# Weight slabs of the first MoE expert placed outside the ring, and an early index spread for the second expert's gather

## The chip, the cores and the metric

The program runs on one NeuronCore of a Trainium2 chip. The metric is the device time of one execution in microseconds (us), the median of the runs shown. The engines are TensorE (PE in the rows; PEld is its weight load), VectorE (DVE), ScalarE (ACT), GpSimd (POOL) and SyncE (SP), which issues the plain DMAs.

## The reference

One decoder block on 512 tokens of width 1024, all in float32. Two attention mixers (NSA and FoX, 8 heads of 64 each) are gated, mixed, projected by `w_out` and added to `x`. Behind them stands a mixture of 32 experts, of which each token takes 4:

```
x = x + mixed @ w_out
h = rms_norm(x, norm2_g)
logits = h @ router_w + router_b          # 32 experts, the 4 best per token, softmax over the 4
hc = h[tokens of e] @ w1[e] + b1[e]       # w1[e] is 1024 x 2048
act = (clip(up) + 1) * gate * sigmoid(1.702 * gate)
y = (act @ w2[e] + b2[e]) * weight        # w2[e] is 1024 x 1024
x = x + sum over the 4 experts of y;  out = rms_norm(x, norm_f_g)
```

All 32 experts are used, so their weights (8.4 MB and 4.2 MB each, 403 MB together) are all read from HBM.

## The kernel before

The kernel is written by hand: each engine has its own instruction list, and semaphores order them. Nothing is scheduled by a planner.

**Stages.** Projections and the two mixers fill the first 440 us. Then eight chunks of mixed heads are gated into `mixT`; PE multiplies them by `w_out` (L1633, eight halves `u` of 512 columns, two for each of the four token tiles `t`), DVE adds `x` (`add_x`, L2109), and the router, the choice of experts and the numbering of slots follow tile by tile. Each expert has room for 96 tokens (`CAP`) in three groups of 32 (`NG`); its first weight is multiplied in `up` (L1673), its second in `down` (L1682 and L1691).

**Weights.** A weight slab is 1 MB (128 x 2048 floats); a pair of slabs is one DMA of 2 MB, issued by SP in `load_pair(e, u)` (L669). `u` = 0 to 3 are the first weight, 4 and 5 the second. They go to the ring, which has places for six pairs. Earlier stages use the ring too: places 4 and 5 hold `w_out` until the last of its matmuls (`out_full`). The first expert uses places 0 to 3 for its first weight; the second expert uses 4, 5, 2 and, as pair (1, 3), the tile `xs` (`RESIDUAL`), which is free once the residual rows are stored; second weights go to places 0 and 1. Pairs are named (expert, u) below, experts counted from 0. A load waits until PE has used what its place held: `w1_used` counts the eight slabs of a first weight, `w2_used` the four steps of a second one. SP issues in the order of its list, and a load that waits holds all behind it.

**The first expert** runs in two passes (`first_expert`), because its first 64 slots come from the first three token tiles: a pass over two groups while the last tile is still being routed, and a pass over the third group. Between the eight steps `c` of the passes PE does routing work: `count_earlier`, `fill_table` (a table of slot, token and gate parts, by one-hot matmuls, L1585; the last tile's in three parts for experts 0 to 3, 4 to 15, 16 to 31), `turn_first_x` (L1625) and `spread_slots` (L1658), which spreads the slot table over the 128 partitions for the gathers.

**The second expert** (`expert(1, 1)`) may start when `rows_ready` and `xT_ready` say so. Its input comes by this chain:

```
DVE take_parts (L2208, L2209)  slot table out of PSUM, after all three parts of the table
PE  spread_slots (L1658)       in the second pass, behind step c = 1
DVE take_quarters (L2194)      indices of all 32 experts
POOL now_gather (L906), gathered (L911), three indirect DMAs of 128 rows x 1 KB
DVE take_x (L2304, L2306)      transpose and scale, then xT_ready
```

On DVE `count_extra` (L2276 to L2292) and `take_gates` (L2214 to L2199, its last instruction gives `rows_ready`) stand between `take_quarters` and `take_x`. Behind them comes DVE's part of the first expert, `expert(0, 0, None)` (L2315 to L2311). From the third expert on, PE's work repeats in one form: `up` of expert e, then `down` of expert e - 1.

Of the kernel before, what the change touches and what calls it, by code (L numbers as in the profile page):

```python
# [7 lines left out]
F32 = mybir.dt.float32  # L8
# [7 lines left out]
P = 128  # L16
S = 512
# [129 lines left out]
def hybrid_block(nc, x, positions, norm1_g, w_in, cmp_pos_emb, cmp_w1, cmp_w2, fox_f_bias, w_proj_nsa,  # L147
                 w_proj_fox, w_out, norm2_g, router_w, router_b, expert_w1, expert_b1, expert_w2,
                 expert_b2, norm_f_g, rope_freqs, out):
    with ExitStack() as ctx:  # L150
# [41 lines left out]
        mix_f = mixT[:, :, :].rearrange("p a b -> p (a b)")  # L192
        probs = mix_f[:, 0:2 * P_LEN].rearrange("p (a b) -> p a b", a=2)
# [26 lines left out]
        pT = sb("pT", [P, 2, P_LEN])  # L220
        pT_f = pT[:, :, :].rearrange("p a b -> p (a b)")
# [7 lines left out]
        rope_cos = sb("rope_cos", [P, S])  # L229
        rope_sin = sb("rope_sin", [P, S])  # L230
# [96 lines left out]
        table_d = nc.dram_tensor("table", (S + 1, D), F32, kind="Internal").ap()  # L327
        x2_d = nc.dram_tensor("x2", (S + 1 + CAP, D), F32, kind="Internal").ap()
# [11 lines left out]
        xn2 = hT_f.rearrange("p (t d) -> p t d", t=NT)  # L340
# [32 lines left out]
        zero_sb = hT_f[0:CAP, 3 * D:4 * D]  # L373
# [68 lines left out]
        RESIDUAL = 6  # L442
        W1_FIRST, W1_SECOND, W1_LATER = (0, 1, 2, 3), (4, 5, 2, RESIDUAL), (4, 5, 2, 3)
        W2_SLOTS, W2_LAST = (0, 1), W1_LATER[0:2]

        def pair_slot(k):

            return xs_f if k == RESIDUAL else ring[:, 2 * k:2 * k + 2, :].rearrange("p c n -> p (c n)")

        def w1_slots(e):  # L450

            return {0: W1_FIRST, 1: W1_SECOND}.get(e, W1_LATER) if isinstance(e, int) else W1_LATER
# [9 lines left out]
        def up_slab(k, h, j):  # L462

            return slab(k, h).rearrange("p (n j m) -> p n j m", n=2, j=4)[:, :, j, :]
# [37 lines left out]
        now_ready = sem("now_ready")  # L502
        xg_loaded = [sem("xg_loaded%d" % b) for b in range(2)]
# [36 lines left out]
        def _(sp):  # L540
# [1948 lines left out]
```

## Time and profile before

| | |
|---|---|
| runs | 1569.91, 1569.84, 1567.62 us; median 1569.84 |
| profiled execution | 1568.18 us, of which the span of the profile is 1566.4 us |
| mean granted TensorE clock | 0.99 of full speed |
| PE busy | 97% of the span |
| DVE, ACT, POOL busy | 38%, 14%, 19% |
| DMA | 464.25 MB, mean 296 GB/s over the span |

The share of a queue or engine is an average over stages with different limits. The span in 40 slices of 39 us shows two parts: up to about 520 us the DMA engines are lightly used, from about 600 us on their share is 0.9 or more in nearly all slices to the end.

### The profile page before, as it was taken

The page shows a single profiled execution, that of the slowest core. Times are in us where ns is not written, and L with a number is a line of the kernel's source. Part 1 is how long each engine was busy: PE and PEld are TensorE (multiplying, and loading weights), DVE is VectorE, ACT ScalarE, POOL GpSimd, SP SyncE. Part 2 cuts the span into 40 slices and gives each one's busy share as a digit, 9 for nine tenths or more (in the row PEclk, how much of TensorE's full clock was granted, in tenths as well). Part 3 has the DMA queues.
Part 4 walks back from the last instruction along what each step waited for, and adds up shares of the span by engine and source line. Part 5 has one row for each costly group of instructions (what it writes and reads, how often), then busy time and mean ns, then how long its engine had stood idle before and what let it go on. Part 6 is the DMA issues. An engine that isn't in the chain of part 4 may idle for free.

```text
span 1566.4 us, 30553 instructions
## 1 busy us (share of the span) xinstructions
PE 1514.1 (97%) x12602; PEld 673.6 (43%) x12603; DVE 595.5 (38%) x1113; ACT 219.2 (14%) x468; POOL 303.0 (19%) x382
## 2 busy tenths in 40 slices
PE   7999999999999989999999999999999999999993
PEld 4655555666445423333333334555553333333331
DVE  4104555333225544235323432442244323432242
ACT  4212444223212100000000000000000000000001
POOL 2000001432100111212222221222121212222111
PEclk9999999999999999999999999999999999999997
DMA  8122130521271699999999999999999999999994
GB/s 240 27 55 54 40 81 14 179 80 31 66 266 68 236 362 398 414 415 420 417 411 418 420 420 412 417 419 416 414 419 417 415 414 417 415 418 408 417 367 138
DMA packets 109421, 464.25 MB, mean 296 GB/s; under 512 B 33683, under 2 KB 72547, under 8 KB 84546
## 3 DMA queue, kind: packets, MB, share of 16 engines
q1 hardware_dynamic: 95506, 446.82, 70.8%
q0 software_dynamic: 13872, 16.83, 4.6%
q8 instruction: 30, 0.49, 0.1%
q14 instruction: 13, 0.11, 0.0%
HBM read 452.94 MB, written 19.29 MB: 301 GB/s over the span
## 4 chain that ended last, share of the span: by engine, by line
PE 77%; DMA 18%; issue 2%; DVE 1%; ACT 1%; ACTq 0%; DVEq 0%; PEld 0%; SPq 0%; PEldq 0%; POOLq 0%
PE ps L1673 32%; DMA ring<-in_expert_w 17%; PE ps L1259 12%; PE ps L1682 10%; PE ps L1409 7%; PE ps L1691 5%; PE ps L1633 4%; PE ps L1394 2%; PE ps L1371 2%; PE ps L1381 2%; ACT mixT L1089 1%; PE ps L1549 0%; DMA xs<-in_x 0%; PE ps L1271 0%; PE ps L1585 0%
## 5 line engine op out<-in xcount | busy, mean ns | idle before, releaser
L1673 PE MATMUL ps<-ring,oT_fox 128*32 128x512 f32 x6096 | 666.7, 594 | 12.2 <-issue 7.8
L1673 PEld LDWEIGHTS ps<-ring,oT_fox 128*32 128x32 f32 x6096 | 225.2, 110 | 427.8 <-issue 396.0
L2315 DVE TENSOR_TENSOR mixT<-ps,mask 128x768 f32<-128x768 f32 x64 | 61.1, 954 | 577.1 <-PE ps L1673 577.1
L1682 PE MATMUL ps<-ring,hT 128*32 128x512 f32 x2048 | 272.3, 592 | 1.3 <-DMA ring<-in_expert_w 1.1
L1691 PE MATMUL ps<-ring,hT 128*32 128x256 f32 x2048 | 163.0, 379 | 0.0
L1691 PEld LDWEIGHTS ps<-ring,hT 128*32 128x32 f32 x2048 | 78.3, 110 | 141.1 <-issue 140.7
L1409 PE MATMUL ps<-hT,ring 128*128 128x512 f32 x304 | 137.2, 598 | 0.0
L911 POOL DMA_INDIRECT oT_nsa<-table,pc x93 | 105.3, 1133 | 47.1 <-POOL pc L906 27.7
L1189 ACT ACTIVATE mixT<-mixT 128x768 f32<-128x768 f32 x32 | 27.1, 846 | 623.5 <-DVE mixT L2319 623.5
L1682 PEld LDWEIGHTS ps<-ring,hT 128*32 128x32 f32 x2048 | 77.1, 110 | 49.8 <-issue 17.5
L1259 PE MATMUL ps<-hT,ring 128*128 128x512 f32 x208 | 90.4, 593 | 0.0
L906 POOL COPY pc<-pc 128x3 int32 (+1 forms) x31 | 8.6, 278 | 412.8 <-DMA x<-hT,v_win 383.6
L1409 PEld LDWEIGHTS ps<-hT,ring 128*128 128x128 f32 x304 | 55.5, 191 | 64.0 <-issue 64.0
L1199 ACT ACTIVATE hT<-pT,v_fox 128x512 f32<-128x512 f32 (+1 forms) x62 | 34.8, 608 | 310.5 <-DVE pT L2351 310.5
L919 POOL COPY v_win<-v_win 128x1 int32 (+1 forms) x64 | 10.2, 186 | 271.8 <-ACT hT L1199 255.6
L931 POOL DMA_INDIRECT x<-hT,v_win x32 | 52.1, 1628 | 42.6 <-POOL v_win L919 25.5
L1089 ACT ACTIVATE mixT<-ps,st 128x128 f32<-128x128 f32 (+1 forms) x96 | 49.1, 536 | 78.3 <-DVE st L1955 78.3
L1259 PEld LDWEIGHTS ps<-hT,ring 128*128 128x128 f32 x208 | 39.1, 190 | 47.7 <-issue 47.6
L1633 PE MATMUL ps<-ring,mixT 128*128 128x512 f32 x128 | 59.4, 602 | 0.0
L2304 DVE STREAM_TRANSPOSE oT_fox<-oT_nsa 128x768 f32<-128x768 f32 x31 | 49.4, 1592 | 11.1 <-DVE mixT L2323 6.6
L924 POOL DMA_INDIRECT x<-hT,v_win x32 | 50.3, 1572 | 9.8 <-issue 9.8
L2311 DVE STREAM_TRANSPOSE hT<-mixT 128x768 f32<-128x768 f32 x32 | 51.1, 1597 | 1.1
(305 smaller groups left out, 1127.3 us busy)
## 6 DMA issues: line engine op xcount, KB each, us to landing
ring<-in_expert_w SPq DMA_DIRECT2D x189, 2048.0 KB
ring<-in_w_in SPq DMA_DIRECT2D x28, 512.0 KB, 4.9
ring<-in_w_out SPq DMA_DIRECT2D x8, 512.0 KB, 9.0
ring<-in_expert_w SPq DMA_DIRECT2D x4, 1024.0 KB, 24.6
ring<-in_w_in SPq DMA_DIRECT2D x1, 2144.0 KB, 12.9
xs<-in_x SPq DMA_DIRECT2D x4, 512.0 KB, 5.5
ring<-in_w_in SPq DMA_DIRECT2D x8, 256.0 KB, 3.5
ring<-in_w_proj_nsa SPq DMA_DIRECT2D x16, 128.0 KB, 2.8
```

The source lines that it names most:

```text
L911: pool.indirect_dma_start(out=xg_rows[b][:, 256 * g:256 * g + 256], out_offset=None, in_=table_quarter, in_offset=bass.IndirectOffsetOnAxi ...
L924: pool.indirect_dma_start(out=x2_quarter, out_offset=bass.IndirectOffsetOnAxis(ap=now_quarter[b], axis=0), in_=yb[b][:, 512:768], in_offse ...
L931: pool.indirect_dma_start(out=x2_half, out_offset=bass.IndirectOffsetOnAxis(ap=now_half[b], axis=0), in_=yb[b][:, 0:512], in_offset=None, ...
L1089: last = act.activation(probs[:, h, P_OFF[t]:P_OFF[t] + P * (t + 1)], scores(h, t), ACT.Exp, bias=ngm[:, h, t:t + 1], accum_out=sums[:, h, ...
L1259: last = pe.matmul(dst, lhs(c), rhs(c), start=(c == 0), stop=(c == n - 1))
L1409: ins = pe.matmul(w, w_c(c), hT[:, c, :], start=(c == 0), stop=(c == NK - 1))
L1633: ins = pe.matmul(ps[:, u, :], mixT[:, k, t * P:(t + 1) * P], w_o[k][:, n * 512:(n + 1) * 512], start=(k == 0), stop=(k == NK - 1))
L1673: ins = pe.matmul(wide(ps[TG * j:TG * j + TG, hc + g, :]), xT[b][:, g, c, :], up_slab(slots[c // 2], c % 2, j), start=(c == 0), stop=(c == ...
L1682: ins = pe.matmul(ps[TG * q:TG * q + TG, bank, :], gT[b][:, q // 2, c, :], rows[:, at:at + 512], start=(c == 0 and bank == Y_BANK), stop=( ...
L1691: ins = pe.matmul(ps[TG * q:TG * q + TG, bank, 0:256], gT[b][:, 2, c, :], rows[:, at:at + 256], start=(c == 0 and bank == Y_BANK + 1), sto ...
L2311: return dve.transpose(gT[b], act_b.rearrange("p g (m c) -> p g c m", c=NK))
L2315: return dve.tensor_tensor(to, half, b_up[:, 256 * n:256 * n + 256].unsqueeze(1).broadcast_to([P, NG, 256]), ALU.add)
```

## The change

- Slabs 4 to 7 of the first expert's first weight no longer go to ring places 2 and 3, but, as four single loads of 1 MB (`load_lone`), to the second half of `hT`, to a new tile `rope_pT` (it holds the rope tables and `pT`, which lay apart before), to half of `mixT` and to half of `xs`. The arrival of each is told by a semaphore that an early stage had used.
- Pairs (1, 2) and (1, 3) go to the ring places 2 and 3 so freed, behind pair (0, 1). (1, 3) no longer uses `xs`. The waits for earlier loads that stood before pairs (1, 0) and (1, 3) are gone. The loads of the third expert all wait for the second expert's use; (2, 3) was loaded ahead of that before.
- `mixT` is laid out by token tile, so that half of it is free after four of the eight halves. `xn2` has two buffers of a tile in place of four. The zero rows behind `table` and `x2` are gone, with the memset and the two small stores that made them.
- `take_parts`, `spread_slots` and `take_quarters` are each cut in two: for experts 0 to 3 in the first pass, once the table's first part is there, and for the others in the second pass as before.
- On DVE the order behind the second `take_quarters` is `take_x`, `take_gates`, a wait for the first expert's last slab, `count_extra`, `expert(0, ...)`.

```diff
+        mix_t = mix_f.rearrange("p (t k m) -> p t k m", t=NT, k=NK)
...
-        pT = sb("pT", [P, 2, P_LEN])
-        pT_f = pT[:, :, :].rearrange("p a b -> p (a b)")
+        rope_pT = sb("rope_pT", [P, 2 * S + 2 * P_LEN])
+        rope_cos, rope_sin = (rope_pT[:, S * n:S * n + S] for n in range(2))
+        pT_f = rope_pT[:, 2 * S:]
...
-        RESIDUAL = 6
-        W1_FIRST, W1_SECOND, W1_LATER = (0, 1, 2, 3), (4, 5, 2, RESIDUAL), (4, 5, 2, 3)
+        W1_FIRST, W1_LATER = (0, 1, 2, 3), (4, 5, 2, 3)
...
+        FIRST_SLABS = slabs_of(W1_FIRST[0:2]) + [hT_f[:, 2 * D:4 * D], rope_pT[:, 0:2 * D], mix_f[:, 0:2 * D], xs_f[:, 0:2 * D]]
+        LONE = 4
...
+            def load_lone(c):
+                src = expert_w1[0].rearrange("e (p c) n -> e p c n", p=P)[0, :, c, :]
+                sp.dma_start(FIRST_SLABS[c], src).then_inc(lone_loaded[c - LONE][0], 16)
...
             load_pair(0, 0)
+            load_lone(4)
+            sp.wait_ge(bias_turned, 1)
+            load_lone(5)
             sp.wait_ge(mix_sig, NK)
-            for u in range(1, 3):
-                load_pair(0, u)
+            load_pair(0, 1)
+            load_pair(1, 2)
             sp.wait_ge(mix_full, NK)
-            load_pair(0, 3)
-            for t in range(NT - 1):
+            load_pair(1, 3)
+            for t in range(EARLY):
                 store_x2(t)
                 store_table(t)
+                if t == 1:
+                    sp.wait_ge(out_full, 4)
+                    load_lone(6)
+                    sp.wait_ge(x2_stored, 16 * 2)
+                    load_lone(7)
             sp.wait_ge(out_full, 2 * NT)
-            for u in range(2):
-                sp.wait_ge(slabs_loaded[u], 16)
             load_pair(1, 0)
-            store_table(NT - 1)
-            store_x2(NT - 1)
+            store_table(EARLY)
+            store_x2(EARLY)
             load_pair(1, 1)
-            sp.wait_ge(x2_stored, 16 * (NT + 1))
-            sp.wait_ge(slabs_loaded[3], 16)
-            sp.wait_ge(xg_loaded[0], 32)
-            load_pair(1, 3)
             for u in range(2):
                 sp.wait_ge(w1_used, 2 * u + 2)
                 load_pair(0, NK // 2 + u)
-            sp.wait_ge(w1_used, 6)
-            load_pair(1, 2)
-            sp.wait_ge(w1_used, 8)
-            sp.wait_ge(slabs_loaded[3], 32)
-            load_pair(2, 3)
-            for u in range(3):
-                sp.wait_ge(w1_used, NK + 2 * u + 2)
-                load_pair(2, u)
...
+            load_w1(2)
             load_w2(1)
...
-            def spread_slots():
-
+            def spread_slots(n):
+
+                first, end = ((0, HOT_PARTS[EARLY][0][1]), (HOT_PARTS[EARLY][0][1], E))[n]
+                pe.wait_ge(parts_taken, n + 1)
...
                     if 4 <= c <= 6:
                         fill_table(EARLY, c - 4)
+                    if c == 5:
+                        spread_slots(0)
                     if c == 6:
                         turn_first_x(1)
...
                     if c == 1:
-                        pe.wait_ge(parts_taken, 1)
-                        spread_slots()
+                        spread_slots(1)
...
             take_first(1)
+            take_parts(0)
             mark(EARLY, 1)
             shift(EARLY)
             mark(EARLY, 2)
+            take_quarters(0)
             dve.tensor_copy(count, routed(EARLY, 2)).then_inc(count_taken, 1)
-            take_parts()
+            take_parts(1)
             take_first_x(1)
...
             weigh(EARLY)
-            take_quarters()
+            take_quarters(1)
+            take_x(1, 1, gather)
+            take_gates()
+            dve.wait_ge(w1_used, NK)
             count_extra()
-            take_gates()
-            take_x(1, 1, gather)
             expert(0, 0, None)
```

Two places in the order of the instructions. A number after a name is the line, `x` the number of instructions of the form.

PE, the end of the first expert's first pass and its second pass, before (`ring` is the weight slab, L1658 is `spread_slots`, L1625 `turn_first_x`, L1585 and L1598 the table):

```order
L1585 MATMUL ps<-v_sel,qk 96x1 x12
L1673 MATMUL ps<-ring,oT_fox 32x512 x8
L1585 MATMUL ps<-v_sel,qk 96x1 x16
L1625 MATMUL ps<-ident,oT_nsa 128x32 x8
L1673 MATMUL ps<-ring,oT_fox 32x512 x16
L1658 MATMUL ps<-v_fox,ident 32x32 x12
L1673 MATMUL ps<-ring,oT_fox 32x512 x12
L1595 MATMUL ps<-kT_win,qk 96x96
L1598 MATMUL ps<-v_sel,qk 96x3 x32
```

and with the change (L1676 is `up`, L1661 `spread_slots`, L1626 `turn_first_x`, L1586 and L1599 the table):

```order
L1586 MATMUL ps<-v_sel,qk 96x1 x4
L1676 MATMUL ps<-rope_pT,oT_fox 32x512 x8
L1586 MATMUL ps<-v_sel,qk 96x1 x12
L1661 MATMUL ps<-v_fox,ident 32x4 x12
L1676 MATMUL ps<-mixT,oT_fox 32x512 x8
L1586 MATMUL ps<-v_sel,qk 96x1 x16
L1626 MATMUL ps<-ident,oT_nsa 128x32 x8
L1676 MATMUL ps<-xs,oT_fox 32x512 x8
L1676 MATMUL ps<-ring,oT_fox 32x512 x8
L1661 MATMUL ps<-v_fox,ident 32x28 x12
L1676 MATMUL ps<-ring,oT_fox 32x512 x8
L1676 MATMUL ps<-hT,oT_fox 32x512 x4
```

A spread of 12 matmuls with 4 columns now stands ahead of the last two steps of the first pass; the old one stays in its place with 28 columns, and the slabs come from `hT`, `rope_pT`, `mixT` and `xs`.

DVE, behind the choice for the last tile, before (L2174 marks one-hots, L2208 and L2209 are `take_parts`, L2194 `take_quarters`, L2276 the start of `count_extra`):

```order
L2174 TENSOR_TENSOR qk<-kT_win 128x1152
L2142 TENSOR_SCALAR kT_sel<-kT_sel,v_win 128x32
L2174 TENSOR_TENSOR qk<-kT_win 128x1536
L2256 COPY kT_win<-ps 128x32
L2208 COPY v_fox<-ps 96x112
L2209 COPY v_fox<-ps 96x16
L2187 TENSOR_TENSOR oT_fox<-ps,v_win 128x256
...
L2156 TENSOR_SCALAR v_sel<-kT_win 128x32
L2194 TENSOR_SCALAR pc<-ps,pc 128x3x32
L2276 TENSOR_SCALAR kT_win<-kT_win 128x1
L2277 SCALAR_TENSOR_TENSOR kT_win<-kT_win 128x1
```

and with the change (L2187 marks one-hots, L2224 is `take_parts`, L2208 `take_quarters`, L2321 and L2323 `take_x`, L2229 the start of `take_gates`):

```order
L2224 COPY v_fox<-ps 96x16
L2187 TENSOR_TENSOR qk<-kT_win 128x1152
L2155 TENSOR_SCALAR kT_sel<-kT_sel,v_win 128x32
L2187 TENSOR_TENSOR qk<-kT_win 128x1536
L2208 TENSOR_SCALAR pc<-ps,pc 128x3x4
L2273 COPY kT_win<-ps 128x32
L2224 COPY v_fox<-ps 96x112
L2200 TENSOR_TENSOR oT_fox<-ps,v_win 128x256
...
L2169 TENSOR_SCALAR v_sel<-kT_win 128x32
L2208 TENSOR_SCALAR pc<-ps,pc 128x3x28
L2321 STREAM_TRANSPOSE oT_fox<-oT_nsa 128x768
L2323 TENSOR_TENSOR oT_fox<-oT_fox,v_win 128x768
L2229 TENSOR_TENSOR v_fox<-v_fox,ps 96x32x3
```

The indices of the first four experts are made in the first pass, and behind the others' `take_x` comes at once, with `take_gates` behind it.

## Rows read from the trace of the kernel before

**Rows 1.** The page, part 2, busy share of the DMA engines in tenths, 40 slices of the span.

```profile
DMA  8122130521271699999999999999999999999994
```

**Rows 2.** Chain that ended last, 480 us to the end: start us, us, what.

```profile
590.80 20.60 PE ps L1673 x192
...
621.72 20.60 PE ps L1673 x192
...
1168.40 26.02 DMA ring<-in_expert_w
...
1456.57 26.29 DMA ring<-in_expert_w
```

**Rows 3.** Windows of 2 us: PE, PEld, DVE, ACT, POOL busy (instructions), PEclk, DMA share, GB/s.

```profile
538.00:540.00 2.00, 2.00 (x20) 1.36 (x24) 1.16 (x6) 0.00 (x0) 0.00 (x0) 1.00 0.62 139
540.00:542.00 2.00, 2.00 (x24) 0.53 (x18) 1.29 (x7) 0.00 (x0) 0.00 (x0) 1.00 0.90 385
...
550.00:552.00 2.00, 0.00 (x0) 0.00 (x0) 0.94 (x4) 0.00 (x0) 1.41 (x2) 1.00 1.02 426
...
556.00:558.00 2.00, 0.32 (x4) 0.23 (x8) 1.97 (x3) 0.00 (x0) 0.00 (x0) 0.50 1.02 418
...
584.00:586.00 2.00, 2.00 (x32) 0.86 (x28) 1.97 (x2) 0.00 (x0) 0.00 (x0) 1.00 0.03 8
```

**Rows 4.** Timeline of SP: start us, us, line, form.

```profile
520.01 0.33 SPq L669 DMA_DIRECT2D ring<-in_expert_w  x1
...
542.70 2.41 SPq L669 DMA_DIRECT2D ring<-in_expert_w  x2
...
564.86 0.33 SPq L669 DMA_DIRECT2D ring<-in_expert_w  x1
...
585.70 0.33 SPq L669 DMA_DIRECT2D ring<-in_expert_w  x1
```

**Rows 5.** Timeline of PE, 530 to 592 us.

```profile
534.49 0.70 PE L1585 MATMUL ps<-v_sel,qk 128*96 128x1 f16 x12
...
538.00 1.06 PE L1625 MATMUL ps<-ident,oT_nsa 32*128 32x32 f32 x8
...
542.45 0.55 PE L1658 MATMUL ps<-v_fox,ident 96*32 96x32 f32 x24
...
557.68 14.85 PE L1673 MATMUL ps<-ring,oT_fox 128*32 128x512 f32 x120 [7.82 <-issue]
```

**Rows 6.** Timeline of POOL, 530 to 600 us.

```profile
533.73 1.47 POOL L890 DMA_INDIRECT oT_nsa<-table,v_win  x1 [8.54 <-DVE v_win L2180]
543.50 0.20 POOL L906 COPY pc<-pc 128x3 int32<-128x3 int32 x1 [8.31 <-DVE pc L2194]
544.58 1.07 POOL L911 DMA_INDIRECT oT_nsa<-table,pc  x1 [0.87 <-POOL pc L906]
...
547.27 1.01 POOL L911 DMA_INDIRECT oT_nsa<-table,pc  x1 [0.30 <-issue]
```

**Rows 7.** Timeline of DVE, 530 to 584 us.

```profile
534.35 1.75 DVE L2174 TENSOR_TENSOR qk<-kT_win 128x1536 f16<-128x1536 f32 x1
...
538.20 0.17 DVE L2209 COPY v_fox<-ps 96x16 f32<-96x16 f32 x1
...
543.07 0.36 DVE L2194 TENSOR_SCALAR pc<-ps,pc 128x96 int32<-128x96 f32 x1 [1.57 <-PE ps L1658]
...
549.76 0.23 DVE L2214 TENSOR_TENSOR v_fox<-v_fox,ps 96x96 f32<-96x96 f32 x1
...
550.86 0.21 DVE L2199 SCALAR_TENSOR_TENSOR v_fox<-v_fox 96x32 f32<-96x32 f32 x1
555.04 1.55 DVE L2304 STREAM_TRANSPOSE oT_fox<-oT_nsa 128x768 f32<-128x768 f32 x1 [3.97 <-DMA oT_nsa<-table,pc]
...
557.50 0.95 DVE L2315 TENSOR_TENSOR mixT<-ps,mask 128x768 f32<-128x768 f32 x1
...
562.65 1.61 DVE L2311 STREAM_TRANSPOSE hT<-mixT 128x768 f32<-128x768 f32 x1
```

More of the change, by code:

```diff
@@ L460, in last_load, with slabs_of, up_slab @@
             return (last_loaded if s % 2 else slabs_loaded)[s // 2], 16
-        def up_slab(k, h, j):
-            return slab(k, h).rearrange("p (n j m) -> p n j m", n=2, j=4)[:, :, j, :]
+        def slabs_of(slots):
+            return [slab(k, h) for k in slots for h in range(2)]
+        def up_slab(rows, j):
+            return rows.rearrange("p (n j m) -> p n j m", n=2, j=4)[:, :, j, :]
+        FIRST_SLABS = slabs_of(W1_FIRST[0:2]) + [hT_f[:, 2 * D:4 * D], rope_pT[:, 0:2 * D], mix_f[:, 0:2 * D], xs_f[:, 0:2 * D]]
+        LONE = 4
         w_mix_loaded = [sem("w_mix_loaded%d" % b) for b in range(2)]
@@ L858, in _ @@
             pool.wait_ge(mix_used, 1)
-            step.link(pool.memset(zero_sb, 0.0))
             for q in range(4):
@@ L957, in _ @@
             block(0, 0, True, 0)
[L958 to L959 removed]
+            pool.wait_ge(x2_stored, 16 * NT)
+            pool.wait_ge(idx_ready, 8)
             with pool.Fori(0, E // 2 - 2) as i:
@@ L1652, in _ @@
                         fill_table(EARLY - 1, 1)
-            def spread_slots():
+            def spread_slots(n):
+                first, end = ((0, HOT_PARTS[EARLY][0][1]), (HOT_PARTS[EARLY][0][1], E))[n]
+                pe.wait_ge(parts_taken, n + 1)
                 for g in range(NG):
                     for q in range(4):
-                        ins = pe.matmul(ps[TG * q:TG * q + TG, SECOND_X, g * E:(g + 1) * E],
-                                        ident[0:CAP, TG * g:TG * g + TG], split[:, :, 0], start=True, stop=True,
+                        ins = pe.matmul(ps[TG * q:TG * q + TG, (FIRST_X, SECOND_X)[n], g * E + first:g * E + end],
+                                        ident[0:CAP, TG * g:TG * g + TG], split[:, first:end, 0], start=True, stop=True,
                                         tile_position=(0, TG * q))
@@ L1665, in wide, with up @@
                 return c.rearrange("p (n m) -> p n m", n=2)
-            def up(b, slots, loaded, used, hc=HC, groups=range(NG)):
+            def up(b, slabs, loaded, used, hc=HC, groups=range(NG)):
                 for c in range(NK):
@@ L1757, in used, with first_loaded @@
                     if c == 1:
-                        pe.wait_ge(parts_taken, 1)
-                        spread_slots()
+                        spread_slots(1)
                     if c == 4:
                         fill_gates()
+                def first_loaded(c):
+                    if c >= LONE:
+                        loaded, value = lone_loaded[c - LONE]
+                        pe.wait_ge(loaded, value + 16)
+                    elif c % 2 == 0:
+                        pe.wait_ge(slabs_loaded[c // 2], 16)
                 pe.wait_ge(xT_ready, 1)
-                up(0, w1_slots(0), lambda c: pe.wait_ge(slabs_loaded[c // 2], 16) if c % 2 == 0 else None, between,
+                up(0, FIRST_SLABS, first_loaded, between,
                    HC_FIRST, range(FIRST // TG))
                 pe.wait_ge(xT_ready, 2)
-                up(0, w1_slots(0), lambda c: None, used, HC_FIRST, range(FIRST // TG, NG))
+                up(0, FIRST_SLABS, lambda c: None, used, HC_FIRST, range(FIRST // TG, NG))
             def second(e, b):
@@ L2097, in _ @@
                 dve.wait_ge(mix_free, c + 3)
-                dve.tensor_tensor(mixT[:, c, :], gate_sig[b][:, 0, :], gate_sig[b][:, 1, :], ALU.add).then_inc(mix_used, 1)
+                sig = [gate_sig[b][:, n, :].rearrange("p (t m) -> p t m", t=NT) for n in range(2)]
+                dve.tensor_tensor(mix_t[:, :, c, :], sig[0], sig[1], ALU.add).then_inc(mix_used, 1)
                 turn_bias(c)
```

74 lines of the change are left out of this document (36 added, 38 removed).

## The prediction

> **What bounds the kernel now.** I read the busy shares by slices first. The DMA engines are nearly idle in the slice from 470 to 509 us (tenth digit 1), at 6 in the next, and at 9 to the end, but for the last slice [rows 1]. So behind 548 us the question is who is late, PE or the weights. The chain that ended last says it: one expert's `up` starts at 590.80 and the next at 621.72 us, with PE alone in the chain, so PE needs 30.92 us for an expert. From 1168.40 us on the chain goes through the arrival of a weight pair, 26 us long, once per expert; from 1168.40 to 1456.57 us there are nine experts, 32.02 us each [rows 2]. The DMA engines thus need 1.1 us more than PE for each expert. What the weights were ahead is used up over the first 19 experts; the last ten follow the DMA engines. The end of the program is the moment from which the weight stream runs without a gap, plus a fixed number of bytes.
>
> When does it begin to run without a gap? SP's list and the windows of 2 us tell. At 584 to 586 us the DMA share is 0.03 [rows 3]: everything that had a place was loaded, and SP waited with pair (1, 4), issued at 585.70 us [rows 4]. That pair goes where `down` of the first expert has just been read. The stream is therefore set by PE at this point, and what I have to find is when PE gets there.
>
> PE stood still before it. It ended the first expert's `up` at 557.68 - 7.82 = 549.86 us and began the second's at 557.68 [rows 5]. At 550 to 552 us it does nothing, at 556 to 558 us its granted clock is 0.50, the lower of its two levels (1.2 GHz), while the DMA share stays at 1.02 [rows 3]. It waited for the second expert's tokens: indices at 543.07 us (L2194), POOL's copy 543.50, the last of three gathers issued at 547.27 us [rows 6], transpose at 555.04 [rows 7], PE 2.64 us behind that.
>
> **The change, part by part.** I call the start of the second expert's `up` T; it was 557.68 us.
>
> *The early spread.* The indices now need only the first part of the table. DVE's extra copy (0.17 us as L2209) stands before the marking; PE's second part of the table began at 534.49 us and took 0.70, and the small spread behind it has half a microsecond (L1658: 0.55 us for 24 passes) [rows 5], so it ends at 535.9. DVE's last marking ends at 534.35 + 1.75 + 0.17 = 536.3 us, the indices at most 0.36 us later, 536.6 instead of 543.4 [rows 7]. POOL is free since 533.73 + 1.47 = 535.2. Its first gather started 1.08 us behind the copy and the third 2.69 us behind the first: third gather at 540.4 us [rows 6]. How long it takes to land has no row in the new surroundings. The nearest are the small gather L890, 4.27 us from its start at 533.73 to its user at 538.00 [rows 5, 6], when the weight queue ran empty, and the same three gathers under full load, 555.04 - 547.27 = 7.77 us [rows 6, 7]. I take 4.3, since SP has nothing to issue before the first expert's second weight (542.70 before, the same condition now) [rows 4]: landed at 544.7, at the latest 548.2.
>
> *DVE's order.* `take_x` and its signal cost 2.64 us: 547.3. `take_gates` now comes behind it, from 549.76 to 550.86 + 0.21 before, 1.31 us [rows 7]; it also needs PE's gate table, which is ready before 548 us. So `rows_ready` comes at 549.3. PE adds the extra spread, 0.55 us [rows 5], and four more waits that are long met: 549.86 + 0.55 = 550.4. PE is the later one by 1.1 us; **T = 550.4 us**, 7.3 earlier. With the late landing T is 548.2 + 2.64 + 1.31 = 552.15.
>
> *The clock.* Without the gap PE keeps the upper level (2.4 GHz). Before, 120 matmuls took 14.85 us [rows 5] where 192 take 20.60 [rows 2], that is 12.88 for 120: 1.97 us more come back.
>
> *`count_extra`* waits for the first expert's last slab and then holds DVE for at most 549.76 - 543.07 = 6.7 us [rows 7]; DVE's part of the first expert behind it takes 562.65 + 1.61 - 557.50 = 6.8 us. It ends at 550.2 + 13.5 = 563.7 us. PE asks for the result after the second `up`, at T + 20.6 = 571.0. It costs nothing: 7 us of cover. Without them every microsecond would show.
>
> *The weights' places.* 4 MB more lie in SBUF when the first expert begins: (1, 2) and (1, 3) are loaded before 475 us, and the single slabs 6 and 7 near 490, where the queue is idle [rows 1]. At 520.01 us SP issues (1, 0) as before. What this is worth I take from the place where the stream became gapless. Before, the ring was full at 583 us although these bytes were still to be loaded; the DMA engines had time for them. So the 4 MB alone are worth nothing. Nor do they cost: (2, 3) is no longer ahead, but all of the third expert's pairs follow PE at 5.15 us each (a quarter of 20.60) [rows 2], the first issued at T + 5.15 + 0.25 = 555.8 us (564.86 before [rows 4], on the slow clock).
>
> *The point that decides.* (1, 4) was issued 585.70 - 557.68 = 28.02 us behind T [rows 4, 5]; without the slow clock 26.05. Now 550.4 + 26.05 = 576.45 us: 9.25 us earlier. The weights before it are the four pairs of expert 2. Issued at 5.15 us each and moved at 5.15 to 5.34 us each (32.02 / 6 [rows 2], with all gathers and scatters in it), they make (1, 4) late by 0 to 0.76 us. I take 0.4. **Gain 8.85 us.** The stores, memset and waits taken out lie where DMA engines and POOL idle: nothing.
>
> *Everything behind* is the same list of loads and the same work on PE. PE's own path moved by 7.3 + 1.97 = 9.3 us, as far as the stream, so neither holds the other back.
>
> The profiled execution took 1568.18 us; 1568.18 - 8.85 = 1559.3. The median of the runs shown is 1.66 us higher, and two of the four times lie up there, two below; I add 0.7: **1560.0 us**. A change within 0.2% (3 us) would be no change by this measurement.
>
> **A rule against it.** The gathers are now issued between 537.7 and 541.4 us beside DVE's small copies, its `tensor_scalar` instructions and its work on gates (busy 1.16 and 1.29 us of the two windows there [rows 3]); before, they ran beside `count_extra`, and took 1.07 and 1.01 us each [rows 6]. If POOL had to wait out each of these instructions of DVE, the last gather would start up to 2.45 us later: landing 547.1, T = 551.1, which costs 0.7 us. The Trainium skill, "SBUF — State Buffer", § Who interferes with whom, says this: a copy or `tensor_scalar` in a two-port mode locks GpSimd out of the port pair it writes descriptors through. No row here shows such a delay; the gathers before ran beside reductions and two-input instructions.
>
> **The rivals.**
> - *Late landing* (or the port): the gathers need as long as under load. For it: the second weight's pairs, 4 MB, are issued from 543 us, before the gathers' data is sure to have come. Against: L890's 4.27 us. T = 552.15 to 553, gain 8.85 - 1.75 to 2.6, that is 1561 to 1563 us. Chance 0.14.
> - *The weights lag more.* The pairs of expert 2, issued one at a time, leave small gaps; each costs once. Between 0.4 and 2 us more: 1560.4 to 1562. For it: in 564.86 to 585.70 us three pairs took all the time there was [rows 4]. This is in the main case's range.
> - *No change.* Another wait fills PE's gap of 7.8 us (for instance the indices still wait for the whole table, or the second `up` for the first's banks). T stays, (1, 4) stays at 585.7, and the 4 MB loaded early give nothing, as reckoned above: 1568 to 1570 us. Against: the new order puts a spread with 4 columns in the first pass. Chance 0.04.
> - *Slower.* `take_gates` now stands behind `take_x`. If the gather lands no earlier than before (555.04), T = 555.04 + 2.64 + 1.31 = 559.0, 1.3 us later than before, and 3 us later if DVE's new order holds up the first expert's result as well: 1569.5 to 1573 us. It decides from a landing at 553.7 us on. For it: nothing but the load on the rings at 545 us. Chance 0.03.
>
> **How the numbers follow.** Main case 0.79: without the extra spread's cost and without lag 1568.18 - 9.8 = 1558.4, and 0.6 less for a low run: 1557.8; with a lag of 2 us and a high run 1562.6. To hold 8 in 10 with the late landing the range goes from 1557.5 to 1564.5. Faster by over 0.2%: the main case and the late landing, 0.93. Same: 0.04. Slower: 0.03.
>
> **What would show it.** PE without a gap of more than 2 us between the first and second expert, granted clock 1.00 throughout; L911's first issue near 537.7 us and `take_x` at 545; SP's pair (1, 4) near 576.5; DMA share 0.9 or more from 560 us on; the first wait for a weight pair still near 1160 us, the period of 32.0 us unchanged. If (1, 4) moves by 9 and the end does not, the stream's rate changed and my fixed number of bytes per time is wrong. If T moves by 7 and (1, 4) by less, places or transfers are late. If T stays, look at which wait ends it.

## The result, and the profile after

| | before | changed |
|---|---|---|
| runs beside each other, median | 1569.88 us | 1560.76 us |
| lowest, highest of four | 1567.62, 1570.06 | 1558.21, 1561.47 |
| profiled execution, span | 1568.18, 1566.4 | 1560.53, 1558.8 |
| granted TensorE clock | 0.99 | 0.99 |

The ratio of the changed kernel to the one before is 0.9943 [0.9927, 0.9958]: 0.57% faster, 9.1 us. The forecast was 1560.0 us, in a range of 1557.5 to 1564.5.

I read the views in the order of the forecast. First POOL, 530 to 560 us, changed kernel:

```profile
533.94 1.54 POOL L889 DMA_INDIRECT oT_nsa<-table,v_win  x1 [8.54 <-DVE v_win L2193]
536.61 0.18 POOL L905 COPY pc<-pc 128x3 int32<-128x3 int32 x1 [1.13 <-DVE pc L2208]
537.67 1.06 POOL L910 DMA_INDIRECT oT_nsa<-table,pc  x1 [0.87 <-POOL pc L905]
539.04 1.02 POOL L910 DMA_INDIRECT oT_nsa<-table,pc  x1 [0.30 <-issue]
540.36 1.01 POOL L910 DMA_INDIRECT oT_nsa<-table,pc  x1 [0.30 <-issue]
```

The copy of the indices stands at 536.61 us, 6.9 earlier than in [rows 6], and the gathers begin at 537.67. DVE, the same stretch:

```profile
536.32 0.22 DVE L2208 TENSOR_SCALAR pc<-ps,pc 128x12 int32<-128x12 f32 x1
...
543.45 0.34 DVE L2208 TENSOR_SCALAR pc<-ps,pc 128x84 int32<-128x84 f32 x1 [1.53 <-PE ps L1661]
543.67 1.60 DVE L2321 STREAM_TRANSPOSE oT_fox<-oT_nsa 128x768 f32<-128x768 f32 x1
545.31 0.96 DVE L2323 TENSOR_TENSOR oT_fox<-oT_fox,v_win 128x768 f32<-128x768 f32 x1
547.57 0.25 DVE L2229 TENSOR_TENSOR v_fox<-v_fox,ps 96x96 f32<-96x96 f32 x1 [1.30 <-PE ps L1599]
...
548.64 0.22 DVE L2214 SCALAR_TENSOR_TENSOR v_fox<-v_fox 96x32 f32<-96x32 f32 x1
550.31 0.15 DVE L2293 TENSOR_SCALAR kT_win<-kT_win 128x1 f32<-128x1 f32 x1 [1.46 <-PE ps L1676]
...
561.88 1.60 DVE L2328 STREAM_TRANSPOSE hT<-mixT 128x768 f32<-128x768 f32 x1
```

The transpose of `take_x` (L2321) has no idle time in front of it, where it had 3.97 us behind the gather before [rows 7]. The tokens lay there when DVE came: at most 543.67 - 540.36 = 3.31 us behind the start of the third gather. `take_gates` (from L2229) waited for PE's table, not for the tokens, and ended at 548.86 us (548.64 + 0.22). Then PE:

```profile
549.20 1.04 PE L1676 MATMUL ps<-xs,oT_fox 128*32 128x512 f32 x8
550.06 13.06 PE L1676 MATMUL ps<-ring,oT_fox 128*32 128x512 f32 x120
...
570.89 1.04 PE L1685 MATMUL ps<-ring,hT 128*32 128x512 f32 x8
```

No idle time stands at 550.06 us, where 7.82 us stood [rows 5], and 120 matmuls take 13.06 us in place of 14.85. PE comes to the first expert's `down` at 570.89; DVE had its input ready at 561.88 + 1.60 = 563.48 us. The windows of 2 us show what this does to the stream of weights:

```profile
542.00:544.00 2.00, 2.00 (x44) 0.84 (x40) 0.55 (x2) 0.00 (x0) 1.29 (x2) 1.00 0.01 0
...
554.00:556.00 2.00, 2.00 (x24) 0.58 (x20) 1.93 (x3) 0.00 (x0) 0.00 (x0) 1.00 0.56 238
...
584.00:586.00 2.00, 2.00 (x24) 0.59 (x20) 0.00 (x0) 0.69 (x2) 0.30 (x2) 1.00 0.91 328
```

PE is busy for the whole of each window, its granted clock 1.00. The DMA engines are idle at 542 to 544 us (share 0.01), where the gathers' data has just come (in steps of 0.5 us their share is 0.04 or less from 541.5 us on, 1.1 us behind the start of the third gather), and have no gap at 584 any more (0.91; 0.03 in [rows 3]). SP issued pair (1, 4) here:

```profile
576.29 0.33 SPq L670 DMA_DIRECT2D ring<-in_expert_w  x1
```

576.29 us in place of 585.70 [rows 4]. Last, the chain of waits:

```profile
581.39 20.60 PE ps L1676 x192
...
612.31 20.60 PE ps L1676 x192
...
1065.99 25.69 DMA ring<-in_expert_w
...
1160.30 26.00 DMA ring<-in_expert_w
...
1448.24 26.34 DMA ring<-in_expert_w
```

PE needs 30.92 us for an expert, and from 1160.30 to 1448.24 us nine experts take 31.99 us each, as before [rows 2]. What moved is when this part begins, not its rate. Two waits for a weight pair stand alone before it, at 1065.99 and 1097.28 us.

### The profile page after: what moved, and what is told of

It reads as the page before. It is cut to its first block, busy times and chain, and to the rows that moved or that the text cites. A ratio compares the mean times of both kernels' runs of the same rounds, so it can differ in the third digit from the quotient of the medians.

```text
span 1558.8 us, 30600 instructions
## 1 busy us (share of the span) xinstructions
PE 1513.6 (97%) x12626; PEld 625.6 (40%) x12627; DVE 595.9 (38%) x1114; ACT 219.0 (14%) x468; POOL 299.5 (19%) x381
## 4 chain that ended last, share of the span: by engine, by line
PE 74%; DMA 21%; issue 2%; ACT 1%; DVE 1%; ACTq 0%; DVEq 0%; SPq 0%; PEld 0%; PEldq 0%; POOLq 0%
PE ps L1676 30%; DMA ring<-in_expert_w 20%; PE ps L1260 12%; PE ps L1685 9%; PE ps L1410 7%; PE ps L1694 4%; PE ps L1634 4%; PE ps L1395 2%; PE ps L1372 2%; PE ps L1382 2%; ACT mixT L1091 1%; PE ps L1550 0%; DMA xs<-in_x 0%; PE ps L1586 0%; DMA oT_nsa<-table,v_win 0%
## 5 line engine op out<-in xcount | busy, mean ns | idle before, releaser
L1676 PE MATMUL ps<-ring,oT_fox 128*32 128x512 f32 x6048 | 658.7, 593 | 4.5 <-DMA ring<-in_expert_w 4.0
L1676 PEld LDWEIGHTS ps<-ring,oT_fox 128*32 128x32 f32 x6048 | 194.8, 110 | 447.6 <-issue 410.4
L1685 PE MATMUL ps<-ring,hT 128*32 128x512 f32 x2048 | 267.8, 592 | 1.5 <-DMA ring<-in_expert_w 1.3
L1694 PE MATMUL ps<-ring,hT 128*32 128x256 f32 x2048 | 158.6, 379 | 0.0
L1694 PEld LDWEIGHTS ps<-ring,hT 128*32 128x32 f32 x2048 | 69.3, 110 | 150.0 <-issue 149.9
L1685 PEld LDWEIGHTS ps<-ring,hT 128*32 128x32 f32 x2048 | 68.2, 110 | 59.0 <-issue 17.8
L1200 ACT ACTIVATE hT<-rope_pT,v_fox 128x512 f32<-128x512 f32 (+1 forms) x62 | 34.7, 607 | 311.0 <-DVE rope_pT L2368 311.0
L2321 DVE STREAM_TRANSPOSE oT_fox<-oT_nsa 128x768 f32<-128x768 f32 x31 | 49.6, 1600 | 7.1 <-DVE mixT L2340 7.1
L923 POOL DMA_INDIRECT x<-hT,v_win x32 | 50.3, 1571 | 9.8 <-issue 9.8
```

Of the source, the lines that this page charges most:

```text
L923: pool.indirect_dma_start(out=x2_quarter, out_offset=bass.IndirectOffsetOnAxis(ap=now_quarter[b], axis=0), in_=yb[b][:, 512:768], in_offse ...
L1676: ins = pe.matmul(wide(ps[TG * j:TG * j + TG, hc + g, :]), xT[b][:, g, c, :], up_slab(slabs[c], j), start=(c == 0), stop=(c == NK - 1), ti ...
L1685: ins = pe.matmul(ps[TG * q:TG * q + TG, bank, :], gT[b][:, q // 2, c, :], rows[:, at:at + 512], start=(c == 0 and bank == Y_BANK), stop=( ...
L1694: ins = pe.matmul(ps[TG * q:TG * q + TG, bank, 0:256], gT[b][:, 2, c, :], rows[:, at:at + 256], start=(c == 0 and bank == Y_BANK + 1), sto ...
```

## The experiments

**How the traces are compared.** Executions of one kernel differ by some us, and much of this arises before the changed stretch. So I count from `a`, SP's issue of pair (1, 0), which both kernels make when the output projection is done. T is the start of the second expert's `up`; `end` is the span. The times of the experiments stand beside runs of the kernel before that were made with them (median 1568.32 us for e1, e2, e3 and e6, 1569.38 for e4, e5, e7 and a2, 1569.58 for e8); each ratio is to those runs and carries its 95% interval. All in us:

| kernel | a | T - a | (1, 4) - a | end - (1, 4) | end - a |
|---|---|---|---|---|---|
| before | 520.01 | 37.67 | 65.69 | 980.7 | 1046.4 |
| before, again (b2) | 518.03 | 37.83 | 66.81 | 980.9 | 1047.7 |
| changed | 520.22 | 29.84 | 56.07 | 982.5 | 1038.6 |
| changed, again (a2) | 518.27 | 29.63 | 55.86 | 982.2 | 1038.0 |
| e1, gather late | 519.08 | 39.11 | 67.73 | 981.9 | 1049.6 |
| e2, weights only | 518.82 | 38.30 | 66.09 | 983.1 | 1049.2 |
| e3, spread only | 518.28 | 32.16 | 60.11 | 981.7 | 1041.8 |
| e4, count first | 522.25 | 33.50 | 61.44 | 982.1 | 1043.6 |
| e5, long count | 518.70 | 29.81 | 64.30 | 980.9 | 1045.2 |
| e6, seventh place | 520.13 | 34.93 | 61.17 | 982.2 | 1043.4 |
| e7, one pair late | 520.18 | 30.94 | 57.19 | 983.1 | 1040.3 |
| e8, seventh later | 518.87 | 30.07 | 56.30 | 982.3 | 1038.6 |

The two kernels again, as a measure of how far this holds:

> The changed kernel once more, beside the others on the same chip: 1560 to 1561.5 us; T 29.8 us and pair (1, 4) 56.1 us behind the issue of pair (1, 0). How far the rest behind (1, 4) differs between executions of the same kernel (982.5 us in the first) tells how much of the 1.8 us that it was longer than before the change is chance.

> The kernel before, a second trace: T 37.7 us, pair (1, 4) 65.7 us and the end 1046.4 us behind the issue of pair (1, 0), whatever its total time is; the issue of (1, 0) itself may lie anywhere from 518 to 522 us, as in the other traces.

The changed kernel came to 1561.13 us, ratio 0.9952 [0.9939, 0.9966]. The one before, profiled once more, took 1567.48 us. The columns behind `a` repeat to 0.6 us for the changed kernel (T and (1, 4) to 0.2, end - a to 0.6) and to 1.3 for the one before. Each experiment has one trace, so about 1 us in (1, 4) or in the end is within this spread.

### The gather late again (e1), and the weights alone (e2)

```diff
-            pool.wait_ge(idx_ready, 3)
+            pool.wait_ge(idx_ready, 4)
             now_gather(1, 1)
```

e1 is the changed kernel with this line: the gather waits for the indices of all experts, as before. e2 has it too, and DVE's old order (`ov` lies in the other half of `mixT` for it, which changes no work):

```diff
             take_quarters(1)
-            take_x(1, 1, gather)
-            take_gates()
-            dve.wait_ge(w1_used, NK)
             count_extra()
+            take_gates()
+            take_x(1, 1, gather)
             expert(0, 0, None)
```

> The changed kernel, but POOL waits for the indices of all 32 experts (made in the second pass) before it gathers for the second expert; weights and DVE's order stay as changed. Theory (the start T of the second expert's up decides, and the early weights are worth nothing alone): indices at 543.8, third gather issued at 547.7, landed 4 to 7 us later beside the second weight's two pairs, take_x and take_gates 3.95 us: T = 556 to 559, pair (1, 4) issued at 584 to 587, time 1567 to 1571 us, likeliest 1569.5, so near the kernel before or a little over it. Rival (4 MB of weights loaded early are the gain, some 10 us of transfer): time stays at 1561 us though T moves.

> As e1, and DVE's old order as well (count_extra, take_gates, take_x; count_extra's scratch lies in the free half of mixT, so it need not wait for the last slab). So only the places of the weights and the split of the spread are left of the change. Theory: T = landing + 2.64, 556 to 557.7, pair (1, 4) at 584 to 585.7, time 1567 to 1569.5 us: about the kernel before. Rival (the weights carry the gain): 1561 us; half of it: 1565.

e1: 1572.23 us, ratio to before 1.0021 [1.0011, 1.0031]. e2: 1571.08 us, 1.0016 [1.0006, 1.0026]. DVE, e1:

```profile
554.41 1.55 DVE L2321 STREAM_TRANSPOSE oT_fox<-oT_nsa 128x768 f32<-128x768 f32 x1 [12.01 <-DMA oT_nsa<-table,pc]
```

and PE, e1:

```profile
558.19 15.44 PE L1676 MATMUL ps<-ring,oT_fox 128*32 128x512 f32 x120 [9.32 <-DVE v_fox L2214]
```

This is the forecast's slower rival made real: DVE stands still for 12 us, waiting for the tokens, with `take_gates` undone, PE starts 3.78 us behind the transpose (the forecast had 2.64 + 1.31 = 3.95), and the clock loss comes back (15.44). In e2 PE starts 2.64 us behind the transpose, as before, and T - a is 38.30:

```profile
554.48 1.55 DVE L2321 STREAM_TRANSPOSE oT_fox<-oT_nsa 128x768 f32<-128x768 f32 x1 [4.62 <-DMA oT_nsa<-table,pc]
```

```profile
557.12 14.62 PE L1676 MATMUL ps<-ring,oT_fox 128*32 128x512 f32 x120 [8.51 <-issue]
```

So the early weights without the early gather gain nothing. Both times lie above what I expected (1567 to 1571 and 1567 to 1569.5 us), a little slower than before, by 0.2%; for e2 the table puts that into end - (1, 4), 983.1 where before has 980.7 to 980.9.

### The spread alone (e3)

The kernel before with `take_parts`, `spread_slots` and `take_quarters` cut in two and DVE's order `take_x`, `take_gates`, `count_extra`; all loads and places as before:

```diff
+            take_parts(0)
             mark(EARLY, 1)
             shift(EARLY)
             mark(EARLY, 2)
+            take_quarters(0)
...
-            take_parts()
+            take_parts(1)
...
-            take_quarters()
-            count_extra()
-            take_gates()
-            take_x(1, 1, gather)
+            take_quarters(1)
+            take_x(1, 1, gather)
+            take_gates()
+            count_extra()
```

> The kernel before with the early spread for the first four experts and DVE's new order, but all weights where they were. T should be 550.4 as in the changed kernel. Theory (the stream needs both: PE's release and no backlog): from 538.9 us eight pairs have to be moved before (1, 4), which took until 582.7 us before; they cannot be done at 576.4, when PE releases (1, 4), so it starts near 582, 4 to 4.5 us earlier than before: 1564.5 to 1567 us, likeliest 1565.5. Rival (T alone decides, the early weights have no part): 1561 us.

1561.84 us, 0.9951 [0.9935, 0.9966]: far more of the gain than I expected, and by the times alone not to be told from the whole change. The traces do tell them apart. POOL, e3:

```profile
535.73 1.06 POOL L911 DMA_INDIRECT oT_nsa<-table,pc  x1 [0.87 <-POOL pc L906]
...
538.42 1.00 POOL L911 DMA_INDIRECT oT_nsa<-table,pc  x1 [0.30 <-issue]
```

DVE, e3:

```profile
546.61 1.61 DVE L2311 STREAM_TRANSPOSE oT_fox<-oT_nsa 128x768 f32<-128x768 f32 x1 [4.85 <-DMA oT_nsa<-table,pc]
```

PE, e3:

```profile
550.44 14.78 PE L1675 MATMUL ps<-ring,oT_fox 128*32 128x512 f32 x120 [2.23 <-DVE v_fox L2204]
```

SP, e3, and its DMA share in windows of 2 us:

```profile
536.41 0.33 SPq L669 DMA_DIRECT2D xs<-in_expert_w  x1
```

```profile
538.00:540.00 2.00, 2.00 (x26) 0.54 (x20) 1.66 (x9) 0.00 (x0) 1.31 (x3) 1.00 0.72 293
540.00:542.00 2.00, 2.00 (x44) 0.81 (x40) 0.34 (x1) 0.00 (x0) 1.23 (x2) 1.00 1.01 428
542.00:544.00 2.00, 2.00 (x23) 0.51 (x16) 0.00 (x0) 0.00 (x0) 1.70 (x2) 1.00 1.09 424
```

In e3 pair (1, 3), 2 MB, is issued at 536.41 us, between the first and the second gather, and the tokens land 8.19 us behind the third one's start, not 3.3. T comes 2.3 to 2.5 us later than in the changed kernel, PE has a gap of 2.23 us and then works at 14.78 us for 120 matmuls, 1.7 more, and (1, 4) is 4.0 to 4.3 us later, the end 3.2 to 3.8. By the times the difference is smaller: about 1 us by the medians (1561.84 beside 1560.76 and 1561.13), 1.8 if each is counted from the runs before beside it for e3 and a2 (6.5 and 8.3 us), and nothing that the intervals part by the ratios (0.9951 beside 0.9943 and 0.9952). So what the places add lies between nothing and 4 us, and only the traces show it.

My expectation had T at 550.4 us and a backlog of weight bytes that holds (1, 4) back to about 582. T came later, and it was PE that released (1, 4), 60.1 us behind `a` (580.1 us, if `a` stood at 520.01 as in the trace before). The backlog is not refuted by that. The DMA share in e3 is 0.96 or more in every window of 2 us from 540 to 578 us, so the stream had no pause to spare, and 0.6 MB were still to come when (1, 4) was released (from the bytes moved behind it, below), 1.5 us at 0.4 MB per us (an estimate). Had PE come 3 to 4 us earlier, 1.8 to 2.2 MB would have been left at the same rate.

### One pair late (e7)

If the landing of the gathers is the reason, the changed kernel with pair (1, 3) issued as late as in e3 must show it:

```diff
             sp.wait_ge(mix_full, NK)
-            load_pair(1, 3)
...
             load_pair(1, 1)
+            sp.wait_ge(xg_loaded[0], 32)
+            load_pair(1, 3)
```

> The changed kernel, but pair (1, 3) is loaded at 538 us, behind the last tile's gather, where it stood before the change (into its ring place). The spread stays early. Theory now (the early weights matter because the queue is empty while the second expert's gathers are in flight, not for their bytes): the gathers land about 8 us behind the third issue in place of 3.3, T comes 2 to 2.5 us later with a gap that lowers the clock (1 to 2 us more), and (1, 4) 3 to 4.5 us later: time 1563.5 to 1565.5 us. Rival (the landing does not depend on weights in flight): T - 0.3 us, time 1560 to 1561.5 us.

1562.32 us, 0.9958 [0.9945, 0.9972]. SP, POOL, DVE and PE, e7:

```profile
538.12 0.33 SPq L670 DMA_DIRECT2D ring<-in_expert_w  x1
```

```profile
537.63 1.07 POOL L911 DMA_INDIRECT oT_nsa<-table,pc  x1 [0.87 <-POOL pc L906]
...
540.32 1.01 POOL L911 DMA_INDIRECT oT_nsa<-table,pc  x1 [0.30 <-issue]
```

```profile
547.29 1.61 DVE L2322 STREAM_TRANSPOSE oT_fox<-oT_nsa 128x768 f32<-128x768 f32 x1 [3.78 <-DMA oT_nsa<-table,pc]
```

```profile
551.12 13.08 PE L1677 MATMUL ps<-ring,oT_fox 128*32 128x512 f32 x120 [1.15 <-DVE v_fox L2215]
```

The landing went from at most 3.31 to 6.97 us, with nothing else changed. T moved by 1.1 to 1.3 us only: between the tokens' arrival and PE's start the changed kernel has about 2.5 us to spare, and a gap of 1.15 us left the clock where it was. (1, 4) came 1.1 to 1.3 us later, the end 1.7 to 2.3. I expected 1563.5 us at least; the slack took the rest. That a weight pair in flight lengthens the flight of the gathers is shown; what it costs depends on the slack.

The pair does not account for all of e3. It stands at the same place there, 0.7 us behind the first gather (0.5 in e7), but the tokens land 8.19 us behind the third gather, 1.2 more than in e7, and why is open. With it PE's gap is 2.23 us in place of 1.15, and the slow clock comes back. So of the 4.0 to 4.3 us by which (1, 4) is later in e3, this run shows 1.1 to 1.3; some 1.2 more are the longer landing and 1.7 the clock. e3 and e7 also differ in the weight bytes loaded ahead, and no run parts these from the landing once the indices come early.

### `count_extra` first (e4), and made long (e5)

e4 is the changed kernel with DVE's old order (the diff of e2) and the early gather kept. e5 repeats four long instructions of `count_extra`:

```diff
+                for _ in range(4):
                     step.link(dve.tensor_tensor(ov[0], ...
                     step.link(dve.tensor_tensor(ov[1], ...
                     step.link(dve.tensor_reduce(ov_e, ov[0], AX.X, ALU.add))
                     step.link(dve.tensor_reduce(ov_s, ov[1], AX.X, ALU.add))
```

> The changed kernel with DVE's old order (count_extra, take_gates, take_x); count_extra's scratch lies in the free half of mixT, and it no longer waits for the last slab. Theory (T, and with it pair (1, 4), decides the end): gathers land by 543.7 as before, but take_x starts only behind 6.3 us of count_extra and 1.3 of take_gates, so T = 554.3 in place of 550.06; a gap of 4 us costs about 2 us more by the lower clock, (1, 4) comes 4 to 6.5 us later, time 1565 to 1567.5 us. Rival (the order on DVE is hidden by PE): 1561 us.

> The changed kernel with the four long instructions of count_extra executed four times (11.9 us more on DVE, same values). Theory: cover is what lies between the first expert's result with the gates' indices (564.8 us) and PE's demand (570.9), 6.1 us; the rest, 5.8 us, becomes a wait of PE before down of the first expert, with up to 2 us more by the clock, and (1, 4) moves by all of it: time 1566.5 to 1569 us. Rival (other weights have slack for it, the stream catches up): under 1563 us.

e4: 1564.34 us, 0.9972 [0.9963, 0.9981]. PE, e4:

```profile
555.75 14.78 PE L1676 MATMUL ps<-ring,oT_fox 128*32 128x512 f32 x120 [3.67 <-issue]
```

T is 3.7 to 3.9 us later, the clock takes 1.7 more, (1, 4) is 5.4 to 5.6 later and the end 5.0 to 5.6: the gathers' tokens lie there and nobody takes them. The early indices are worth their full gain only with DVE's new order. By the medians of this comparison (before 1569.38 us) 5.0 of the changed kernel's 8.3 us are left, so the loss is 3.2 us by the medians, less than by the trace, and the time is a little under the 1565 us expected. The profiled execution of e4 is one of its longer ones: seven of the eleven took 1563.5 to 1564.6 us, four, with this one (1567.55), 1566.7 to 1568.8; what parts them is open.

e5: 1567.41 us, 0.9987 [0.9978, 0.9996]. The waits of PE behind 540 us, e5:

```profile
PE ps L1685 <- issue: 5.6, 1, 5.6
```

T - a is that of the changed kernel, but PE waits 5.6 us before `down`, (1, 4) is 8.2 to 8.4 us later and the time 6.3 longer. The 2.6 us above the wait go with the slow clock: granted 0.50 in the windows from 574 to 580 us. `count_extra` is 11.9 us longer here (three more rounds of four instructions, 3.96 us each). So the cover was 11.9 - 5.6 = 6.3 us, near the 7 of the forecast, and past it DVE sets the point that matters.

### A seventh place for weights (e6, e8)

`xs`, 2 MB, stays unused once the first expert has read its slab. e6 makes it a place for the last pair of every second expert, so that 2 MB more can be ahead. The lines that matter at 530 us (`load_half(1)` loads slab 7 of expert 2, 1 MB, to `xs`, and `load_half(0)` its slab 6):

```diff
             load_pair(1, 1)
+            sp.wait_ge(x2_stored, 16 * NT)
+            load_half(1)
...
+            sp.wait_ge(w1_used, NK)
+            load_half(0)
```

e8 adds `sp.wait_ge(xg_loaded[0], 32)` before `load_half(1)`.

> The changed kernel with xs kept as a seventh place for the rest of the program: slabs 6 and 7 of every even expert from the third on go there, one half of pair (2, 3) from 533 us on, the other at 550 us, and (e + 2, 3) is issued when expert e has used its own. Theory (the end is the moment from which the stream runs without a gap plus a fixed number of bytes; the gaps at 536 to 544 and 554.5 to 557 us are lack of places): 2 MB more are moved in these gaps, up to 5 us: 1555.5 to 1558.5 us, likeliest 1556.5, and the first wait for a weight pair comes later than 1160 us. Rival (the rate near the end or PE's path is what bounds, or the half slabs delay the gather): 1560 to 1562 us.

> As e6, but the half pair for xs is issued at 538 us, behind the landing of the last tile's gather, so it cannot delay it. Theory (T decides; what is loaded ahead of its turn is worth nothing, since pair (31, 3) then stands before (31, 0), for which PE waits at the end): T about 1 us later than in the changed kernel, as in e7, all else alike: 1561 to 1563.5 us, pair (1, 4) 57 us and the end 1039 to 1041 us behind the issue of pair (1, 0). Rival (the 2 MB more that lie in the chip before the stream has no gap any more bring their 5 us): 1555.5 to 1558.5 us.

e6: 1565.27 us, 0.9975 [0.9965, 0.9986], above my range and above the rival's; the changed kernel has 1560.76 and 1561.13. SP, POOL and PE, e6:

```profile
531.49 0.33 SPq L682 DMA_DIRECT2D xs<-in_expert_w  x1
```

```profile
533.86 1.54 POOL L918 DMA_INDIRECT oT_nsa<-table,v_win  x1 [8.54 <-DVE v_win L2227]
```

```profile
540.78 1.08 PE L1655 MATMUL ps<-ident,oT_nsa 32*128 32x32 f32 x8 [2.62 <-DMA oT_nsa<-table,v_win]
541.80 3.64 PE L1705 MATMUL ps<-xs,oT_fox 128*32 128x512 f32 x16
```

The slab stands ahead of the small gather of the last token tile: PE waits 2.62 us for it, and its next 16 matmuls take 3.64 us in place of 1.92 (the granted clock is 0.50 in the windows from 542 to 546 us, the level of 1.2 GHz). The wait that the kernel before had at this place for its pair (1, 3), and that the change could drop because nothing is loaded there, guards against just this. With the wait back (e8) 1559.72 us, 0.994 [0.9927, 0.9954], under the 1561 us expected but not in the rival's range, and end - a 1038.6, that of the changed kernel: 2 MB more ahead bring nothing that can be told from noise. The lead itself was there: behind (1, 4) 393.3 MB are moved in e8, 394.9 in the changed kernel. I had expected it to be lost because pair (31, 3) stands ahead of (31, 0), for which PE would wait at the end. The trace of e8 has no such wait. Its last wait of PE for a weight is this one, for the second weight of expert 28:

```profile
1447.22 1.06 PE L1715 MATMUL ps<-ring,hT 128*32 128x512 f32 x8 [0.81 <-DMA ring<-in_expert_w]
```

That `down` starts 928.4 us behind `a`, and 928.0 in the changed kernel. SP's list says why the lead does not help there: with the seventh place the fourth pair of the next expert, (30, 3), is issued ahead of (28, 4), so that PE's next weight has one more pair before it. This is argued from the list; no run tried another order.

## Why the prediction was right, and where it was off

- **What bounds it.** "A moment from which the stream runs without a gap, plus a fixed number of bytes": end - (1, 4) stays within 980.7 to 983.1 us in twelve traces, while (1, 4) - a goes from 55.86 to 67.73. Of the alternatives named as signs, neither came: (1, 4) moved by 9.41 us and the profiled time by 7.65. e8 limits the sentence: 1.6 MB fewer are left behind (1, 4) there and end - (1, 4) is 982.3 all the same, so it is the order of the pairs that is fixed, not their bytes alone.
- **Luck in the single figures.** The forecast's times count from the trace before, with `a` at 520.01 us, and the profiled execution of the changed kernel happened to have 520.22. In a2 it is 518.27, and T (547.90) and (1, 4) (574.13) come 2.5 and 2.3 us ahead of the forecast. The fair comparison is behind `a`: T - a 29.8 and 29.6 (forecast 30.4), (1, 4) - a 56.1 and 55.9 (56.4).
- **Indices and gathers.** 536.61 us (forecast 536.6), first gather 537.67 (537.7), third 540.36 (540.4). The landing was taken at 4.3 us from L890 and is at most 3.3. L890's 4.27 us was a gather that began while the queue was still full (DMA share 0.95 at 534 to 536 us), so it was no measure of an empty queue; that it served is luck. e3 and e7 show why the choice between the two rows was the right one: with weights in flight it is 7.0 to 8.2 us, without them it is short. The late landing was a real rival, kept out by the place of the loads. Its T of 552.15 for a landing of 7.8 us is that of e3 (T - a 32.16; 552.15 - 520.01 = 32.14); what it left out is the slow clock behind the gap. It agrees although e3's landing is 8.2 us, because two smaller terms go the other way.
- **T.** 550.06 (550.4), and, as forecast, PE set it: `rows_ready` stood at 548.86 (549.3).
- **The clock.** The forecast had 1.97 us come back; 1.79 did.
- **`count_extra`.** 7 us of cover forecast; e5 gives about 6.
- **(1, 4).** 576.29 (576.45).
- **"The 4 MB alone are worth nothing."** Right alone (e2). Beside the early spread (1, 4) comes 4.0 to 4.3 us earlier with the new places (changed and a2 against e3). 1.1 to 1.3 us of it are shown to come from the queue that is empty while the gathers fly (e7); for the rest see the section on e7. This part of the gain was in my sum, inside the landing of 4.3 us, and I gave it to the wrong edit. That the bytes ahead have no share in it is not shown.
- **The lag of the pairs of expert 2** is the term that was mis-sized: 0.4 taken, 0 to 0.76 allowed. The end came 1.8 us (a2: 1.5) less forward than (1, 4). In the three traces where the stream stood idle just before (1, 4) (before, b2, e5) end - (1, 4) is 980.7 to 980.9, in the nine others 981.7 to 983.1. So a stream that is released pair by pair by PE reaches that point 1 to 2 us behind the one that was ahead and waited. The bytes say the same. From the issue of (2, 0) to that of (1, 4) the changed kernel moves 381 GB/s x 20.83 us = 7.9 MB; e5, where the same transfers were all through before (1, 4), moves 301 GB/s x 29.09 us = 8.8 MB:

```profile
555.46:576.29 20.83, 20.83 (x228) 7.04 (x224) 13.59 (x24) 1.69 (x2) 3.22 (x4) 1.00 0.97 381
```

```profile
553.91:583.00 29.09, 23.46 (x228) 7.64 (x224) 27.81 (x39) 1.69 (x2) 3.22 (x4) 0.88 0.77 301
```

So 0.8 MB were still to come at (1, 4) in the changed kernel, 2 us at 0.4 MB per us (an estimate). Summed over windows of 2 us from (1, 4) to the end it is the same: 394.1 MB in before, b2 and e5, 394.7 in e3, 394.9 in changed, a2, e1, e2, e4 and e7. Part of it is won back, since the stream of before has to start from nothing at (1, 4): in the first 20 us behind it the changed kernel moves 0.3 MB more. My formula had only the mean time of a pair over the whole stream. What it gave in favour of a lag, that three pairs took all the time there was [rows 4], was misread: the DMA share before is 0.26 at 582 to 584 us and 0.03 in the next window [rows 3], so the pairs were through by 583 us. With 1.8 in place of 0.4 the sum is 1561.4; the median of 1560.76 lies between. Why e2 and e7 have 983.1 with the same bytes is open.
- **The rule on the port.** POOL's three instructions took 1.06, 1.02 and 1.01 us beside DVE's small instructions, as beside `count_extra` before (1.07 and 1.01). The delay that the Trainium skill, "SBUF — State Buffer", § Who interferes with whom, would let one expect for copies and `tensor_scalar` in a two-port mode does not show here; whether any of these instructions ran in such a mode the trace does not say.
- **The first late weight pair.** Two waits now stand alone, at 1065.99 and 1097.28 us (one in a2, at 1094.75); the regular ones begin at 1160.30, as foreseen. What made the early ones stays open. The two traces of the kernel before differ in this too: the first wait stands at 1168.40 us in one and at 1136.37 in b2.

## What to carry to other kernels

When a stream of loads bounds the end, find the last instant at which it had nothing to do, and who released it: only what moves that instant moved the end here. Bytes loaded before it did nothing alone (e2), nor did one more place for them in the order tried (e8). Then look which small transfer the releasing engine waits for, and keep the large queue empty while it flies: a slab of 1 MB issued 2.4 us ahead of a small gather cost 5 us and brought nothing (e6). An engine order that parks long work in front of the thing awaited gives back much of such a gain (e4), and behind it the parked work has a limited cover (e5).

## What the runs showed of the hardware

- The same three gathers (128 rows of 1 KB each) were there at most 3.3 us behind the third one's start with the weight queue empty (changed, a2, e5). With one pair of 2 MB issued between the first and the second they took 7.0 us (e7) and 8.2 us (e3), with one issued ahead of the first 7.8 to 8.5 us (before, b2, e1, e2). In all six, one or more further pairs were issued before the tokens landed.
- A gap of PE of 1.15 us left 120 matmuls at 13.08 us (e7); gaps of 2.23 (e3) and 3.67 us (e4) were followed by 14.78, gaps of 7.8 to 9.3 us (before, b2, e1, e2) by 14.62 to 15.80. Against 13.06 the short gaps cost 1.7 us, the long ones 1.6 to 2.7.
- The time `a`, ahead of which these kernels do the same work, moves between 518.03 and 522.25 us from one execution to the next. A comparison of two single profiles of this kernel is worth less than the same comparison counted from `a`.
